# Second head's chunk maps of an RWKV-7 recurrence in the other partition half, by identity products

## The reference, cut to what matters

```
def _rwkv7_step(state, inp):
    r, w, k, v, kk, a = inp
    sa = einsum("dbhvk,dbhk->dbhv", state, kk)
    state = state * w[..., None, :] - sa[..., None] * (kk * a)[..., None, :] + v[..., None] * k[..., None, :]
    return state, einsum("dbhvk,dbhk->dbhv", state, r)
```

## Time and profile before

| what | us |
|---|---|
| median of 3 runs (lowest, highest) | 6700.87 (6697.97, 6701.71) |
| span of the profiled execution (its time outside the span is not on the page) | 6691.4 |
| TensorE busy, matmuls | 5726.3 |
| VectorE, ScalarE, GpSimd busy | 2945.0, 2000.7, 1877.3 |

### The profile page before, as it was taken

How to read it: one execution, slowest core, us unless ns; L and a number is a source line. 1 busy time by engine, 2 the same in 40 slices (tenths; PEclk the granted TensorE clock), 3 DMA queues, 4 the chain that set the end, 5 groups by cost and what they waited for, 6 DMA issues and landing times. The chain is left out here.

```text
span 6691.4 us, 214952 instructions
## 1 busy us (share of the span) xinstructions
PE 5726.3 (86%) x92840; PEld 3836.5 (57%) x92840; DVE 2945.0 (44%) x6319; ACT 2000.7 (30%) x3323; POOL 1877.3 (28%) x2006
## 2 busy tenths in 40 slices
PE   5999888888887799977887885689799888888887
PEld 4555577777774355445554453544354477777773
DVE  6200266666662233135533377520310366666661
ACT  1000255555440222133422132310100254555440
POOL 4452144444441335100001641000000244444440
PEclk8999999999998899988898997899899899999998
DMA  3222100001102322122212236523112100011002
GB/s 125 89 96 82 50 31 31 31 33 43 37 31 85 121 76 97 46 85 64 62 48 103 97 104 92 122 73 115 52 68 75 47 31 31 31 44 39 31 31 91
DMA packets 196092, 441.22 MB, mean 66 GB/s; under 512 B 24769, under 2 KB 108609, under 8 KB 195649
## 3 DMA queue, kind: packets, MB, share of 16 engines
q1 hardware_dynamic: 160896, 338.58, 17.0%
q10 hardware_dynamic: 34752, 96.51, 3.6%
HBM read 329.14 MB, written 105.87 MB: 65 GB/s over the span
## 5 line engine op out<-in xcount | busy, mean ns | idle before, releaser
L356 PE MATMUL ps<-arena 128*128 128x512 f32 x4544 | 1683.6, 532 | 73.1 <-DMA arena<-s_w_in 27.4
L356 PEld LDWEIGHTS ps<-arena 128*128 128x128 f32 x4544 | 862.3, 190 | 889.7 <-issue 853.9
L1875 PE MATMUL ps<-arena 64*64 64x64 f32 x35840 | 741.3, 225 | 164.2 <-DVE arena L2542 66.1
L153 POOL TENSOR_TENSOR arena<-arena 128x512 f32<-128x512 f32 (+1 forms) x360 | 330.6, 935 | 1782.7 <-DMA arena<-w_mod 1772.5
L1875 PEld LDWEIGHTS ps<-arena 64*64 64x64 f32 x35840 | 646.8, 138 | 237.9 <-issue 223.9
L2280 ACT COPY arena<-ps 128x512 f32<-128x512 f32 (+1 forms) x880 | 536.0, 627 | 426.6 <-PE ps L1875 418.3
L2425 POOL TENSOR_TENSOR arena<-arena 128x256 f32<-128x256 f32 (+1 forms) x320 | 318.5, 1002 | 807.7 <-DVE arena L2666 528.9
L570 PE MATMUL ps<-arena 128*128 128x512 f32 (+1 forms) x1152 | 424.2, 528 | 33.5 <-DMA arena<-na_w_in 33.5
L2350 POOL MEMSET arena<- 128x1280 f32 (+4 forms) x22 | 15.1, 739 | 1370.6 <-POOLq L83 1370.6
L1631 DVE SCALAR_TENSOR_TENSOR arena<-arena 128x1280 f32<-128x1280 f32 (+3 forms) x120 | 147.2, 1299 | 567.2 <-PE ps L356 477.1
L156 POOL TENSOR_TENSOR arena<-arena 128x256 f32<-128x256 f32 (+2 forms) x504 | 381.8, 769 | 52.0 <-issue 2.1
(11 more groups left out here) (258 smaller groups left out, 9853.6 us busy)
## 6 DMA issues: line engine op xcount, KB each, us to landing
arena<-proj SPq DMA_DIRECT2D x158, 640.0 KB, 5.1
proj<-arena ACTq DMA_DIRECT2D x80, 640.0 KB, 4.0
arena<-w_mod SPq DMA_DIRECT2D x96, 512.0 KB, 7.6
arena<-rw_w SPq DMA_DIRECT2D x68, 512.0 KB, 3.7
arena<-xres SPq DMA_DIRECT2D x40, 640.0 KB, 6.7
xres<-arena ACTq DMA_DIRECT2D x24, 640.0 KB, 6.0
arena<-na_w_in SPq DMA_DIRECT2D x24, 512.0 KB, 3.5
arena<-x SPq DMA_DIRECT2D x16, 640.0 KB, 6.6
```

The source lines that it names most:

```text
L153: self.nc.gpsimd.tensor_tensor(out, strip[:, c:c + n, :], self.k.cond[:, c:c + n, s:s + 1].to_broadcast([P, n, P]), ALU.mult)
L356: last = nc.tensor.matmul(k.ps[:, 3 * u + n, 0:b - a], w[:, c * P:(c + 1) * P], src[:, c, a:b], start=(c == 0), stop=(c == KT - 1))
L1875: last = PE.matmul(part_of(out, dst, hh, g, d), part(l, src, hh, g, d), rhs, start=True, stop=True)
```

## The change

The second head's token maps are left in the other half. Results and operands are moved accordingly: the result half of r-scores and kh-scores, of the transposed values, kh and beta, and of L2044 becomes c ^ hh; L2006 reads from c ^ hh and writes to c; transfers, gains and local outputs read from c ^ hh. A 128-wide transpose can't put the two heads into different halves, so it is replaced by 64-row products with the identity (`turn_chunks`). The loop of L2044 goes over hh inside of q instead of outside.

```diff
-            tiles = [(c, HP[c], hh, HP[hh]) for hh in range(2) for c in range(2)]
+            tiles = [(c, HP[c ^ hh], hh, HP[hh]) for hh in range(2) for c in range(2)]
...
+            def turn_chunks(out, col, between, in_, crossed):
+                for g in range(2):
+                    for hh in range(2):
+                        for c in range(2):
+                            at, to = (2 * g + c) * C, col + g * between
+                            last = PE.matmul(out[HP[c ^ (hh & crossed)], hh, to:to + C], in_[HP[hh], at:at + C], k.eye2[HP[hh], :],
+                                             start=True, stop=True)
+                return last
...
-                scores(low[1], BH_, R_).then_inc(m4_mm, 1)
+                scores(low[1], BH_, R_, 1).then_inc(m4_mm, 1)
                 pe.wait_ge(v_kept, it + 1)
-                for g in range(2):
-                    PE.transpose(bank[7][:, g * P:(g + 1) * P], v_win[:, g * P:(g + 1) * P], k.ident)
-                    for d in range(2):
-                        last = PE.transpose(bank[6][:, (g * 2 + d) * P:(g * 2 + d + 1) * P], ops[:, KK_, d, g * P:(g + 1) * P], k.ident)
+                hold(k, pe)
+                turn_chunks(high[3], 0, C, v_win, 1)
+                for d in range(2):
+                    last = turn_chunks(low[3], d * C, 2 * C, ops[:, KK_, d, :], 0)
                 last.then_inc(kv_mm, 1)
...
                 pe.wait_ge(m3_ev, it + 1)
+                hold(k, pe)
                 for n, kind in enumerate((KH_, BH_)):
-                    for g in range(2):
-                        for d in range(2):
-                            last = PE.transpose(bank[4 + n][:, (g * 2 + d) * P:(g * 2 + d + 1) * P],
-                                                ops[:, kind, d, g * P:(g + 1) * P], k.ident)
+                    for d in range(2):
+                        last = turn_chunks(pair[2], (4 * n + d) * C, 2 * C, ops[:, kind, d, :], 1)
                 last.then_inc(kb_mm, 1)
...
-                                last = PE.matmul(part_of(low[3], c, hh, g, d), part(M1, c, hh, g, d), Vt[HP[c], g, HP[hh]],
+                                last = PE.matmul(part_of(low[3], c, hh, g, d), part(M1, c ^ hh, hh, g, d), Vt[HP[c ^ hh], hh, g * C:(g + 1) * C],
                                                  start=True, stop=True)
...
-                for hh in range(2):
-                    for g, d, q in pairs:
+                for g, d, q in pairs:
+                    for hh in range(2):
                         for c in range(2):
-                            last = PE.matmul(bank[4 + hh][HP[c], q * P:(q + 1) * P], part(F, c, hh, g, d), RH[HP[c], hh * 4 + q, :],
+                            last = PE.matmul(bank[4 + hh][HP[c ^ hh], q * P:(q + 1) * P], part(F, c, hh, g, d), RH[HP[c], hh * 4 + q, :],
                                              start=True, stop=True)
...
-                    SC.copy(flat(Vt), bank[7][:, 0:2 * P])
+                    SC.copy(Vt, high[3][:, :, 0:2 * C])
                     SC.copy(RH[:, :, 0:C].rearrange("p (h q) c -> p h q c", h=2),
-                            bank[6].rearrange("p (q h c) -> p h q c", h=2, c=C)).then_inc(kv_ev, 1)
+                            low[3].rearrange("p h (q c) -> p h q c", c=C)).then_inc(kv_ev, 1)
```

More of the change, by code:

```diff
@@ L1876, in product, with kt, bt @@
                 return last
-            tiles = [(c, HP[c], hh, HP[hh]) for hh in range(2) for c in range(2)]
+            tiles = [(c, HP[c ^ hh], hh, HP[hh]) for hh in range(2) for c in range(2)]
             pairs = [(g, d, g * 2 + d) for g in range(2) for d in range(2)]
[L1881 to L1885, removed]
+            def kt(cp, hh, q):
+                return KB[cp, hh, q * C:(q + 1) * C]
+            def bt(cp, hh, q):
+                return KB[cp, hh, (4 + q) * C:(5 + q) * C]
+            def turn_chunks(out, col, between, in_, crossed):
[6 more added lines that the diff above has]
+                return last
             def transfers():
@@ L1889, in transfers @@
                     for c, cp, hh, hp in tiles:
-                        PE.matmul(bank[4 + c][hp, q * C:(q + 1) * C], RH[cp, hh * 4 + q, 0:C], bt(cp, q, hp),
+                        PE.matmul(bank[4 + c][hp, q * C:(q + 1) * C], RH[cp, hh * 4 + q, 0:C], bt(cp, hh, q),
                                   start=True, stop=True)
@@ L1895, in gains @@
                     for c, cp, hh, hp in tiles:
-                        PE.matmul(bank[4 + c][hp, (4 + q) * C:(5 + q) * C], kt(cp, q, hp), Vt[cp, g, hp], start=True, stop=False)
+                        PE.matmul(bank[4 + c][hp, (4 + q) * C:(5 + q) * C], kt(cp, hh, q), Vt[cp, hh, g * C:(g + 1) * C], start=True, stop=False)
                     for c, cp, hh, hp in tiles:
-                        last = PE.matmul(bank[4 + c][hp, (4 + q) * C:(5 + q) * C], bt(cp, q, hp),
+                        last = PE.matmul(bank[4 + c][hp, (4 + q) * C:(5 + q) * C], bt(cp, hh, q),
                                          RH[cp, hh * 4 + q, C:2 * C], start=False, stop=True)
@@ L1908, in local_outputs @@
                     for c, cp, hh, hp in tiles:
-                        PE.matmul(bank[2 + c][hp, g * C:(g + 1) * C], Vt[cp, g, hp], part(M3, c, hh, g, 0), start=True, stop=False)
+                        PE.matmul(bank[2 + c][hp, g * C:(g + 1) * C], Vt[cp, hh, g * C:(g + 1) * C], part(M3, c ^ hh, hh, g, 0), start=True, stop=False)
                     for d in range(2):
@@ L1912, in local_outputs @@
                             PE.matmul(bank[2 + c][hp, g * C:(g + 1) * C], RH[cp, hh * 4 + g * 2 + d, C:2 * C],
-                                      part(M4, c, hh, g, d), start=False, stop=(d == 1))
+                                      part(M4, c ^ hh, hh, g, d), start=False, stop=(d == 1))
                 for g, d, q in pairs:
@@ L1916, in local_outputs @@
                         last = PE.matmul(bank[2 + c][hp, (2 + q) * C:(3 + q) * C], RH[cp, hh * 4 + q, 0:C],
-                                         part(M4, c, hh, g, d), start=True, stop=True)
+                                         part(M4, c ^ hh, hh, g, d), start=True, stop=True)
                 last.then_inc(yq_mm, 1)
@@ L1960, in window @@
                                 at, col = (2 * g + c) * C, (g * 2 + d) * C
-                                last = PE.matmul(halves(pair[2][HP[c], hh, :])[:, :, col:col + C], ops[HP[hh], KH_, d, at:at + C],
+                                last = PE.matmul(halves(pair[2][HP[c ^ hh], hh, :])[:, :, col:col + C], ops[HP[hh], KH_, d, at:at + C],
                                                  ops[HP[hh], KK_:R_ + 1, d, at:at + C], start=True, stop=True)
```

## The result

The changed kernel takes 7679.51 us (7668.27 to 7687.71, 4 runs) against 6699.42 us (6696.94 to 6701.71, 4 runs) for the kernel before: ratio 1.1462, 95% interval 1.1447 to 1.1477. Slower by 980 us, where 84 us less were forecast.

A forecast was written before the change was run, and what follows sets the result against it. A chain changing engines from one window's L2044 to the next was taken to bound the kernel, not TensorE's busy time. Gains of 43.7, 21.0 and 19.4 made 84 us: 6617 us, range 6590 to 6660 (0.85).

The forecast's parts named there:

- Rates: TensorE's 64-row products: 14.5 ns apart on all four quarters of the array, 28.7 ns on two (L2006).
- part 1: L2044 on four quarters: 1.98 to 1.10 us; 0.48 passes on for n=1 to 3, 0.88 for n=4, 0.78 in tails.
- Part 2: Transposes of values, kk, kh and beta become identity products at 14.5 ns an instruction: gain 0.43 us in every window.
- Part 3: L2006 on four quarters: 1.02 to 0.59 us, but this 0.43 is worth nothing to the path.
- cover: Behind L2006, z2 products wait for VectorE's L2666 anyway; without that wait the gain would be 34 us more.
- Part 4: Quarter order in transfers, gains and local outputs, copies from other banks, added waits: all taken to cost nothing.
- The sum's third line: 16 first windows with the tail before them, 0.78 + 0.43 us each: 19.4 us gained.
- The clock: TensorE's clock falling inside windows would show the forecast wrong; the sum allowed 8 us over 16 tiles, for tails.
- D: Row halves sharing a bank stall transfers, gains and local outputs: +116 us, 6817; chance 0.05.
- E: Identity products run at 28.7 ns: +36 us, 6737; chance 0.04.

The follow-up runs named there:

- e3: Changed kernel with three groups of 16 products (L2006's w, z2, z4) cut to one each, part of the computation left out; 6689.03 us, ratio 0.9985.
- e4: Kernel before with L2006 and L2044 on four quarters, 128-wide transposes kept, second head crossed in copies by other engines; 6672.22 us, ratio 0.9964.
- e5: Kernel before with more filling, the window loop 24 instructions later in the first layer and 48 in the second; 6716.85 us.
- e2: Kernel before with F's identity product repeated once more a window in the first RWKV layer (1749 instructions), three times more in the second (1877); 7397.55 us.
- e1: Kernel before with the first layer's window loop moved by 128 instructions of filling, the second's place in its block kept; 7223.82 us against 6697.97.
- e6: Kernel before with the identity product done twice in both layers (1749 instructions), loop 40 instructions earlier in the first, 7 later in the second; 6770.73 us against 6693.35.

## Why the prediction was wrong

By its own steps:

- **Rates and part 1, L2044.** Right. 1.98 became 1.10 (e3 and e4: 1.11). In windows 1 to 3 the products of xt start 0.12 behind the mask (852.44 to 852.56 in e3), and from them to x4 it is 854.88 - 852.56 = 2.32 us, the number of the sum. For n = 4 e3's window is 17.74, forecast 17.7; the best of n = 1 to 3 are 18.1 for a forecast of 18.4 (e3 also saves TensorE the cut groups, so its windows do not measure this part alone).
- **Part 2, turns.** Right where the code is resident: r-scores to identity product 1.17 (forecast 1.22), from there to z 1.49 (1.46), in e3.
- **Part 3, L2006.** Its cover was as said; with w cut to one product, z2t at 863.18 still waits 0.98 us, for the negation on VectorE (the old L2666) to end at 863.12. Not separated from the other cuts.
- **Part 4, edits at nothing.** This is the step that failed: "no engine but TensorE issues another number of instructions", and TensorE's 98 more pairs a window were charged 14.5 ns each and nothing more. I costed instructions by the time that they take on the array. They also take room, and the loop had some 26 instructions of it left by the estimate above (24 fitted in e5, 64 did not in e2), for 198. That cost 12 us in each of the three windows n = 1 to 3 of a first-layer tile and 15 in its last, 15 and 17.5 in the second layer. The trace of before showed the signs: 304 code packets of 16 KB on the page, none in steady windows, 14 in each tail with its first window, and pauses called "issue" in mid-group there, as this one in the first window of the second tile, which the prediction does not speak of:

```profile
973.78 0.86 PE L1875 MATMUL ps<-arena 64*64 64x64 f32 x43 [2.12 <-issue]
```

And the kernel carries 147 and 17 empty increments ahead of its recurrences, which compute nothing; e1 shows what they set, the place of the code.
- **The sum's third line** (first window with the tail, 0.78 + 0.43) would have failed even with resident windows: e3 shows +1.5 instead of -1.2, since what the tail gains (-1.4) is lost again in the first window (+2.9), where its own longer code is fetched and TensorE stops with a code packet on its way; that the fetch is all of the 2.9 is argued, not shown. With it the forecast for resident windows would be 84 - 43 = 41 us. e3's recurrences are 31 us shorter. That the two are near is luck: e3 saves TensorE the cut groups, and it loses 28 us to the clock.
- **The clock** was among the signs of being wrong, but the sum has it only in the tails, with 8 us either way. In e3, where TensorE idles more, it fell in 24 of 64 windows and cost 28 us. Whether it would in the complete kernel with a resident loop no run here shows.
- **Rivals.** D named the right size of trouble for a wrong reason, and the experiments exclude it; likewise E. None of the six named code. The range held no case for it.

The Trainium skill, "Runtime: NRT & Kernel Launch", section "Instruction fetch mechanics", says that TensorE's instruction memory holds 2048 instructions, is refilled in blocks of 256 that the sequencer fetches by its own DMA queue, and that crossing a block border is mostly hidden. The packets of 16 KB and their own queue (14.63 MB in 893 packets) and the 126 or 127 pairs between two stops agree with it. That the cost is hidden does not: at the array's rate TensorE issues 256 instructions, 128 pairs, in 1.9 us (128 x 14.5 ns), the code packets start 3.5 to 3.9 us apart, and the stops shown lose about the difference, 1.3 to 1.9 us, the one at the start of a round 3.5 us; a resident window loses none. And a loop of 1883 instructions, fewer than 2048, did not stay.

Open: whether seven blocks is the limit or eight with one always given to what comes next; why a loop on the edge is fetched in every second round; why nine blocks are fetched in a round also where the loop touches eight, as in e1 and in the changed kernel's first layer; and why the same nine packets go with 31 us a window in its first layer and 35 in its second.

## What to carry to other kernels

Before you add instructions to a loop that runs in tens of microseconds, count what one round issues and look at the instruction queue: no code packets inside the loop means that it is resident, and that its length is a budget. A change that saves array time by more, smaller products can lose the whole loop's residency; exchange layout in copies that are made anyway instead, as e4 does. When TensorE idles on "issue" in the middle of a group of equal products, look for code packets before you look at the data path.

## What the runs showed of the hardware

- A TensorE loop of 1685 instructions is resident at its places in both layers, 24 instructions later in the first and 48 later in the second; 128 later in the first it is not. One of 1749 is resident at one place and alternates 40 instructions further on; loops of 1877 and 1883 never are (e1, e2, e5, e6).
- A non-resident round costs 9 packets and, in the medians, 31 to 37 us, whatever its content: 31.2 us at 1877 instructions, 33 at 1685 (19.3 us when resident). Its time follows the packets, which start 3.5 to 3.9 us apart, and not the work.
- The stops in such a round lie 126 or 127 pairs of load and matmul apart: a 16 KB packet holds 256 instructions.
- 64x64 float32 products on four quarters start 14.5 ns apart also where both row halves write one bank: transfers 0.59 us for 32 instructions with either order.
- In e3, where TensorE idles more in a window, its granted clock is 0.98 over the first tile's last four windows. It was 0.50 for 3.4 us, after stops of at most 0.9 us, and 32 loads of L1862 took 1.06 us there instead of 0.59:

```profile
866.40:869.80 3.40, 3.40 (x128) 3.31 (x124) 2.01 (x6) 1.13 (x2) 2.11 (x3) 0.50 0.00 0
832.90:905.70 72.80, 60.57 (x3348) 57.38 (x3341) 50.73 (x90) 45.41 (x86) 37.20 (x43) 0.98 0.09 31
```
